# Making the attention's queries one block at a time, in twelve short matmuls, instead of half the sequence at a time in three long ones

## The reference, cut to what matters

```
def block(args):                       # one block of 128 queries, all 1024 keys
    q_blk, i = args
    qpos = (i * Q_BLOCK + jnp.arange(Q_BLOCK)).astype(jnp.float32)
    bias = -slopes[:, None, None] * jnp.abs(qpos[:, None] - kpos[None, :])
    s = jnp.einsum('bqhmd,bkhmd->bhmqk', q_blk, k,
                   preferred_element_type=jnp.float32) * scale + bias[None, :, None]
    p = jax.nn.softmax(s, axis=-1)
    w = p[:, :, 0] - lam * p[:, :, 1]
    return jnp.einsum('bhqk,bkhe->bqhe', w.astype(v.dtype), v)
```

## Time and profile before

| | |
|---|---|
| median of three runs | 2966.4 us (2963.76 to 2967.34) |
| the profiled execution's own time | 2963.76 us |
| its span in the profile | 2962.0 us |
| PE busy | 2761.2 us, 93% of the span |
| DVE busy | 1571.1 us, 53% |
| ACT busy | 983.5 us, 33% |
| mean granted clock of PE | 0.964 of full |

### The profile page before, as it was taken

One profiled execution on the slowest core, in us unless ns is written; L12 is line 12 of the kernel. 1 busy time (PEld: TensorE's weight loads), 2 busy tenths in 40 slices (PEclk: granted clock), 3 DMA queues, 4 the chain that ended last, 5 costly groups with the idle time before them and its releaser, 6 DMA issues. The chain is left out here.

```text
span 2962.0 us, 38767 instructions
## 1 busy us (share of the span) xinstructions
PE 2761.2 (93%) x15744; PEld 2278.4 (77%) x15744; DVE 1571.1 (53%) x2476; ACT 983.5 (33%) x1829; POOL 300.7 (10%) x260
## 2 busy tenths in 40 slices
PE   6999998999898799998989879998899999999998
PEld 3788887778865699777879758866588888888887
DVE  4302456777642612456767553868844444444445
ACT  3201232555521411233555424248732122112112
POOL 0000001321431000001312420000000000000001
PEclk7999998999999899998999989999999999999999
DMA  6321122005454221122025341100210101101102
GB/s 263 97 86 54 52 86 77 12 15 190 151 215 160 106 84 60 59 79 64 12 89 168 110 187 47 39 29 1 114 36 29 52 34 57 57 28 57 57 31 90
DMA packets 109143, 239.71 MB, mean 81 GB/s; under 512 B 9698, under 2 KB 65044, under 8 KB 100672
## 3 DMA queue, kind: packets, MB, share of 16 engines
q1 hardware_dynamic: 87840, 222.85, 21.7%
q10 hardware_dynamic: 21152, 14.75, 1.6%
HBM read 194.57 MB, written 42.99 MB: 80 GB/s over the span
## 5 line engine op out<-in xcount | busy, mean ns | idle before, releaser
L920 PE MATMUL ps<-xn_hi_sb,ft_hi_sb 128*128 128x512 f32 x720 | 268.0, 372 | 10.6 <-DVE ft_lo_sb L1355 10.6
L921 PE MATMUL ps<-xn_lo_sb,ft_hi_sb 128*128 128x512 f32 x720 | 263.2, 366 | 0.0
L922 PE MATMUL ps<-xn_hi_sb,ft_lo_sb 128*128 128x512 f32 x720 | 263.0, 365 | 0.0
L2955 DVE TENSOR_TENSOR arena_sb<-arena_sb,ps 128x512 f32<-128x512 f32 x256 | 172.9, 686 | 121.5 <-PE ps L2634 118.8
L868 PE MATMUL ps<-tm_hi_sb,xn_hi_sb 128*128 128x512 f32 (+2 forms) x608 | 215.7, 355 | 0.8 <-DVE xn_lo_sb L1282 0.8
L870 PE MATMUL ps<-tm_hi_sb,xn_lo_sb 128*128 128x512 f32 (+2 forms) x608 | 213.3, 351 | 0.0
L869 PE MATMUL ps<-tm_lo_sb,xn_hi_sb 128*128 128x512 f32 (+2 forms) x608 | 213.0, 350 | 0.0
L2593 PE MATMUL ps<-xn_hi_sb,w_up_hi_sb 128*128 128x512 f32 x512 | 199.3, 389 | 0.0
L2595 PE MATMUL ps<-xn_hi_sb,w_up_lo_sb 128*128 128x512 f32 x512 | 199.2, 389 | 0.0
L2594 PE MATMUL ps<-xn_lo_sb,w_up_hi_sb 128*128 128x512 f32 x512 | 199.2, 389 | 0.0
L2632 PE MATMUL ps<-w_down_hi_sb,h_hi_sb 128*128 128x512 f32 x480 | 186.7, 389 | 0.0
(11 more groups left out here) (414 smaller groups left out, 6196.6 us busy)
## 6 DMA issues: line engine op xcount, KB each, us to landing
arena_sb<-in_w_ft SPq DMA_DIRECT2D x44, 512.0 KB, 3.6
arena_sb<-mqk_dram SPq DMA_DIRECT2D x36, 512.0 KB, 3.4
arena_sb<-x_dram SPq DMA_DIRECT2D x33, 512.0 KB, 5.9
arena_sb<-in_w_ada SPq DMA_DIRECT2D x16, 1024.0 KB, 9.6
arena_sb<-in_w_up SPq DMA_DIRECT2D x16, 1024.0 KB, 6.5
arena_sb<-in_w_down SPq DMA_DIRECT2D x16, 1024.0 KB, 4.9
arena_sb<-in_xall SPq DMA_DIRECT2D x20, 512.0 KB, 4.8
arena_sb<-mv_dram SPq DMA_DIRECT2D x40, 256.0 KB, 3.9
```

The source lines that it names most:

```text
L920: pe.matmul(to, hi, xn_hi_flat[:, k, at:at + size], start=k == 0, stop=False)
L921: pe.matmul(to, hi, xn_lo_flat[:, k, at:at + size], start=False, stop=False)
L922: mm = pe.matmul(to, lo, xn_hi_flat[:, k, at:at + size], start=False, stop=k == KT - 1)
```

## The change

A query unit is cut the other way. `queries(b, j)` now makes four planes (heads 2j and 2j+1, both maps) for one block of 128 queries. It still fills one PSUM bank with 4 by 128 columns, but each of the four pieces has its own three matmuls of 128 columns: twelve instead of three. The bias rows come from 32 contraction rows (of which 16 are zero) in place of 16. ACT still copies 112 x 512 elements per unit. There are again 16 units, now two for each block, all in bank 7. `q2_st` shrinks to two alternating buffers of one block each.

The units are made just in time: unit (b+1, h) stands at the end of steps h = 0 and h = 1 of block b, for b = 0 to 6. Unit (0, 0) is made in the projections, ahead of the last projection tile, and the wait there asks for one more key copy (`rep_ev` 6 for 5), since the unit's bank is one from which that copy reads. Unit (0, 1) stands behind the scores of step 0. The constants `alibi_q` and `alibi_sel` change shape (48 x 512 and 48 x 128 become 128 x 128 and 128 x 256), and the arena shrinks from 51880 to 51400 columns.

```diff
...
     out["alibi_k"] = np.concatenate([side == 0, (side == 0) * (pos - P * tile)], 0).astype(f)
     rows = np.concatenate([-side * (pos - P * tile), side + 0 * pos], 0)
-    out["alibi_q"], out["alibi_sel"] = np.zeros((48, SEQ // 2), f), np.zeros((48, P), f)
-    for half in range(2):
-        at = slice(32 * half, 32 * half + 2 * NX)
-        out["alibi_q"][at] = rows[:, SEQ // 2 * half:SEQ // 2 * (half + 1)]
-        out["alibi_sel"][at, TERMS:ROWS2] = np.eye(2 * NX)
+    out["alibi_q"] = rows.reshape(2 * NX, NX, P).transpose(1, 0, 2).reshape(P, P).astype(f)
+    place = np.arange(P)[:, None, None] % 32 == 16 * np.arange(2)[None, :, None] + np.arange(P)[None, None, :] - 96
+    out["alibi_sel"] = (place & (np.arange(P) >= 96) & (np.arange(P) < 96 + 2 * NX)).astype(f)
...
-        ARENA = 51880
+        ARENA = 51400
...
         prob2 = [[part(W2 + 2048 * u + 1024 * m, SEQ) for m in range(2)] for u in range(2)]
         w_t = [[part(at + 1024 * g, NX, P) for g in range(2)] for at in (YT + 4096, M2 + 2048)]
-        q2_st = rounded("q2_st", XNT, 8, SEQ)
-        q_base_raw, q_base = apart("q_base_raw", M2 + 18592, SEQ // 2), rounded("q_base", M2 + 18592, SEQ // 2)
+        q2_st = [rounded(f"q2_st{u}", W2 + 4096 + 1024 * u, 8, P) for u in range(2)]
...
         alibi = sb("alibi", [P, P], F16)
-        q_place_raw, q_place = sb("q_place_raw", [48, P]), sb("q_place", [48, P], F32R)
+        q_base_raw, q_place_raw = sb("q_base_raw", [P, P]), sb("q_place_raw", [P, 2, P])
+        q_base, q_place = sb("q_base", [P, P], F32R), sb("q_place", [P, 2, P], F32R)
...
             N_CV, N_KQ, N_C = 0, 4, 8
-            QUERY = 4 * (7, 6) + 8 * (7,)
             F2_TILES = 10
...
                     repeat_keys(6)
                     pe.wait_ge(c_ev, 1)
                     repeat_keys(7)
-                    pe.wait_ge(rep_ev, 5)
+                    pe.wait_ge(rep_ev, 6)
+                    queries(0, 0)
                     ft_tile(N_C + 1)
 
                 def repeat_keys(n):
@@ -2395,27 +2393,29 @@
                         mm = pe.matmul(at, rep_k[rows, 1, 0:TERMS], kq_lo[0][rows, n // 4, 512 * c:512 * (c + 1)], start=False, stop=True)
                     mm.then_inc(rep_mm, 1)
 
-                def queries(i):
-                    half, j, r = i // 8, i % 8 // 4, i % 4
-                    if i >= 2:
-                        pe.wait_ge(d_q, i if i > 8 else i - 1)
-                    cols, side, at = slice(512 * half, 512 * (half + 1)), slice(32 * half, 32 * half + 2 * NX), ps[:, QUERY[i], :]
-                    pe.matmul(at, rep_q[:, r, 0, :], kq_hi[1][:, j, cols], start=True, stop=False)
-                    pe.matmul(at, rep_q[:, r, 1, :], kq_lo[1][:, j, cols], start=False, stop=False)
-                    pe.matmul(at, q_place[side, :], q_base[side, :], start=False, stop=True).then_inc(q_mm, 1)
+                def queries(b, j):
+                    if b == 0 and j == 0:
+                        pe.wait_ge(rep_round, 2)
+                    cols, side = slice(b * P, (b + 1) * P), slice(32 * (b // 2), 32 * (b // 2) + 32)
+                    for r in range(4):
+                        at = ps[:, 7, r * P:(r + 1) * P]
+                        pe.matmul(at, rep_q[:, r, 0, :], kq_hi[1][:, j, cols], start=True, stop=False)
+                        pe.matmul(at, rep_q[:, r, 1, :], kq_lo[1][:, j, cols], start=False, stop=False)
+                        mm = pe.matmul(at, q_place[side, b % 2, :], q_base[side, :], start=False, stop=True)
+                    mm.then_inc(q_mm, 1)
...
                     def scores(s, b, u, h, m):
-                        if b % 4 == 0:
-                            pe.wait_ge(d_q, 2 * b + 2 * h + m + 1)
+                        if h % 2 == 0 and m == 0:
+                            pe.wait_ge(d_q, 2 * b + h // 2 + 1)
                         if s > 0:
                             pe.wait_ge(d_e[m], s)
                         for c in range(2):
                             own = c == b // 4
-                            mm = pe.matmul(ps[:, 2 * m + c, :], q2_st[0:ROWS2, 2 * h + m, b * P:(b + 1) * P], k2_st[0:ROWS2, 2 * h + m, 512 * c:512 * (c + 1)],
+                            mm = pe.matmul(ps[:, 2 * m + c, :], q2_st[u][0:ROWS2, 2 * h + m, :], k2_st[0:ROWS2, 2 * h + m, 512 * c:512 * (c + 1)],
                                            start=True, stop=not own)
...
@@ -2459,19 +2459,15 @@
                                 values(b, 0, h - 2)
                             elif not first:
                                 values(b - 1, 1, h)
-                            if s == 0:
-                                queries(6)
-                                queries(7)
-                            if 4 <= s < 12:
-                                queries(4 + s)
+                            if h < 2 and not last:
+                                pe.wait_ge(d_q, 2 * b + 2 + h)
+                                queries(b + 1, h)
 
                     for h in range(2):
                         for m in range(2):
-                            queries(2 * h + m)
-                        for m in range(2):
                             scores(h, 0, 0, h, m)
-                    queries(4)
-                    queries(5)
+                        if h == 0:
+                            queries(0, 1)
                     pe.wait_ge(c_ev, 2)
                     each(NX, query_block)
...
                     act.wait_ge(const2, CONST2_ALL)
-                    act.activation(q_base[0:48, :], q_base_raw[0:48, :], ACT.Copy)
-                    act.activation(q_place[:, :], q_place_raw[:, :], ACT.Copy).then_inc(rep_round, 1)
+                    act.activation(q_base[:, :], q_base_raw[:, :], ACT.Copy)
+                    act.activation(q_place[:, :, :], q_place_raw[:, :, :], ACT.Copy).then_inc(rep_round, 1)
...
                     channels(0)
                     for n in range(4, 8):
                         keys(n)
+                    queries(0, 0, 0)
                     channels(1)
 
-                def queries(i):
-                    half, r = i // 8, i % 8
-                    act.wait_ge(q_mm, i + 1)
-                    act.activation(q2_st[0:ROWS2, r, 512 * half:512 * (half + 1)], ps[0:ROWS2, QUERY[i], :], ACT.Copy).then_inc(d_q, 1)
+                def queries(b, u, j):
+                    act.wait_ge(q_mm, 2 * b + j + 1)
+                    act.activation(q2_st[u][0:ROWS2, 4 * j:4 * j + 4, :].rearrange("p r q -> p (r q)"), ps[0:ROWS2, 7, :], ACT.Copy).then_inc(d_q, 1)
...
@@ -3160,22 +3156,15 @@
                             if h < 2 or not last:
                                 exp(s + 2, *((u, h + 2) if h < 2 else (1 - u, h - 2)), 0)
                             evacuate(s, h)
-                            if s == 0:
-                                queries(6)
-                                queries(7)
-                            if 4 <= s < 12:
-                                queries(4 + s)
+                            if h < 2 and not last:
+                                queries(b + 1, 1 - u, h)
                             if h == 1 and b > 0:
                                 attended(b - 1)
 
+                    queries(0, 0, 1)
                     act.wait_ge(sub_ready, 1)
-                    for i in range(4):
-                        queries(i)
                     for h, m in ((0, 0), (0, 1), (1, 0)):
-                        if h == 1:
-                            queries(4)
                         exp(h, 0, h, m)
-                    queries(5)
                     each(NX, query_block)
                     attended(NX - 1)
```

More of the change, by code:

```diff
@@ L2165, in second_block @@
             first2, FIRST2_ALL = sem("first2"), 16 * len(FIRST2)
-            CONST2 = [(alibi[:, :], "alibi"), (slope, "slope"), (q_base_raw[0:48, :], "alibi_q"), (q_place_raw[:, :], "alibi_sel"), (pw_w, "pw_w"), (fnet_w, "fnet_w"), (dft_c, "dft_c"),
+            CONST2 = [(alibi[:, :], "alibi"), (slope, "slope"), (q_base_raw[:, :], "alibi_q"), (q_place_raw[:, :, :], "alibi_sel"), (pw_w, "pw_w"), (fnet_w, "fnet_w"), (dft_c, "dft_c"),
                       (sgu_rows, "sgu_rows"), (sgu_w, "sgu_w"), (dw_w, "dw_w"), (dw_b, "dw_b"),
```

## The result

The changed kernel takes 2988.85 us in the median of four runs (2985.29 to 2993.82), against 2965.08 before: a ratio of 1.0083 (95% interval 1.0064 to 1.0101), 0.64% to 1.01% slower. The forecast was +18 us. The direction held, and so did the price of a unit; the size of the loss did not. On 2966.4 us, the median of before that the forecast had, the ratio gives 2991 us. That is 9 more than the 2982 forecast, which started 2.6 lower, from the profiled execution, and it is above the upper end of the range, 2989 (the bare median, 2988.85, stands at that end, beside a before that was 1.3 lower in the same runs). The profiled execution took 2986.52 us, its span is 2984.7, and the last combination of the attention comes at 2135.83 instead of 2113.07. That is 22.76 us, and the whole span is 22.7 longer.

A forecast was written before the change was run, and what follows sets the result against it. It took a step to be bound by a loop between DVE and ACT, with little cover on PE. 25.2 + 2.2 + 0.5 - 8.6 - 0.7 = +18.6, taken as +18: 2963.8 + 18 = 2982 us, range 2968 to 2989.

The forecast's parts named there:

- The unit's cost: On PE, a query unit of twelve short matmuls takes 2.5 us instead of 1.09, bias loads not being hidden.
- Rival A: Short matmuls' loads are pulled ahead, a unit takes 1.34 us: +1.6 us, 2965 us, not slower; chance 0.12.
- The block with values: Attention blocks 1 to 6: two steps with units make each block 4.2 us late, nothing caught up; 25.2 us.
- What went away: Attention of the kernel before: units and clock cost 5.6 + 3.0 = 8.6 us, which the change removes.
- The start: Projections to first combination: unit (0, 0) pushes the tile 3.35 us, yet the first combination gains 0.7 us.
- the scores could start at 1967.0: Start of the attention: 1963.67 plus the tile's 3.35 us delay; before, scores started at 1966.95 behind two units.
- Clock 1.00 from block 1 on: Attention: PE's granted clock was expected to stay full in all blocks from 1 on.
- the 0.5 us in block 0: Block 0: 0.5 us added to its 2.2 us lateness for the lower clock that fell there before.
- rival B: Blocks with units: PE's waits for loads lower the clock, unit 3.6 us, +19 on top, 3001 us; chance 0.06.
- The argument against B: Attention before: clock was 1.00 in all steps from 2 on, also where PE waits 0.75 us in each.

The follow-up runs named there:

- full rows: Changed kernel with the bias matmul contracting over all 128 rows instead of 32, same order: 2968.78 us, 1.0019 to the kernel before.
- POOL's copy and the other place together: Changed kernel without bias matmuls (POOL copies the bias rows), later units between the turn and the scores of map 1: 2954.72 us, 0.9970 to before.
- the copy alone: Changed kernel without bias matmuls, POOL copying the 16 bias rows into `q2_st`, units where they were: 2963.63 us, 0.9999 to before.
- full rows with the other place: Changed kernel with bias matmuls over 128 rows and later units between the turn and the scores of map 1: 2959.47 us, 0.9995 to before.
- other place: Changed kernel with later units moved from behind the values to between the turn and the scores of map 1: 2986.57 us, 1.0086 to before.

## Why the prediction was right and wrong

- **The unit's cost** (2.5 us forecast, 2.48 measured) was right, and so was the reason: full rows shows that equal row counts hide the loads. Rival A, which took the hidden loads from the earlier trace rows, had the right price for them (1.34; measured 1.39) but not the case. Its sum was +1.6 us. Full rows came out 5.5 above its own before (2968.78 to 2963.31), and its trace 3.9 counted from the keys: the steps with a unit are 1.06 and 1.22 late instead of 1.0, which makes 1.4 in six blocks, and block 0 is 0.95 late instead of 0.1. Its start gained the 1.9 that rival A had for it, and there the tile ran at the full clock.
- **The block with values** (4.2 us) was right to 0.1 us in five of six blocks, through both paths: the unit's copy ahead of the exponential, and the next scores behind the unit. Steps without a unit take 4.15, so that nothing is caught up, and the mixers absorb nothing.
- **What went away** (8.6 us) was right.
- **The start failed.** This is the first of the two steps that failed. The prediction had a gain of 0.7; it was a loss of 0.84. The wait and the unit were right to 0.2 us. The step "the scores could start at 1967.0" took the tile at the full clock, and it ran at 0.60 for its first 3.8 us. Behind it `neg_lam` came at 1971.41 instead of 1969.8, and the first maximum, which waited for it on DVE, at 1971.61.
- **The clock failed.** "Clock 1.00 from block 1 on" was wrong, and the 0.5 us in block 0 was 1.3. Of the 4.2 us between the forecast sum (18.6) and the profiled one (22.8) 4.1 lie in stretches where the granted clock was under 1: 1.5 at the start, 0.8 in block 0, 1.75 in block 3. The forecast's sum had the clock only as the 0.5. For the blocks rival B named the mechanism and gave it 0.06 for all twelve steps; what happens is between the two, a dip of 1 to 2 us in one or two blocks of an execution and a low clock in block 0. The argument against B, that the clock was 1.00 in every step from 2 on also where PE waited 0.75, was a bad one. It took one kind of gap for another: a wait between full-pace stretches had not lowered the clock, and that told nothing of a stretch in which matmul after matmul waits for its load. For the 1.5 us at the start B's mechanism is not what the runs show: the tile's clock fell as well behind units with hidden loads (0.55 and 0.57).
- The rest of the 9 us between 2982 and 2991 is 2.6 for the lower time that the forecast started from, 0.6 for rounding 18.6 to 18, and 1.8 between the profiled 22.8 and the ratio (24.6 on 2966.4). The last is within what executions differ by: the second profile of the changed kernel has its last combination 6.2 us later than the first, 2.9 of it from ahead of the keys and the rest at the start and in the dips.

What stays open: why the clock falls at the tile when a unit stands ahead of it, and why not in the one trace of full rows; why it falls at the start of the attention in every kernel, the one before and those with hidden loads too; and what decides in which block it dips. The runs varied only the unit's form and place ahead of the attention, not the wait for the key copy or the tile.

## What to carry to other kernels

Before cutting a matmul into shorter ones, look at the loads between them. Where neighbours contract over 128 and over 16 or 32 rows, each change cost a fixed time here that the long matmul paid once, and then columns are not what you count. Give all matmuls of a group the same rows or hand the odd one to another engine, and put the unit where the critical loop has slack. Only POOL's copy and the other place together came out clearly faster than the kernel before (0.9970); the copy alone (0.9999) and full rows with the other place (0.9995) did not. And when short pieces with unhidden loads replace long ones, add a term for the clock in the blocks where they stand, and one where a wait and a unit are put ahead of other work, not only where it fell before.

## What the runs showed of the hardware

- In the rounded fp32 format a matmul of 128 columns with 128 rows takes 0.112 us in a stream with its load, twice the 128 / 2400 = 0.053 of its columns. A change from 128 rows to 32 and back adds about 0.27 us, one from 128 rows to 112 nothing that shows (full rows), and one from the products with the values (loads of 64 columns) to loads of 128 columns 0.06.
- An engine that counts as busy for a whole step can keep the full clock (full rows, other place: 4.62 of 4.62 us, 1.00) or lose it (other place: 6.98 of 6.98, 0.76). The busy share does not tell them apart.
- POOL's copy of 16 x 1024 elements takes 1.04 to 1.76 us in the attention, against 1.01 ahead of it, where DVE waits. It slows nothing that can be seen: the steps around it take 4.14 to 4.15 us.
